# Layer seams worked one token block after the other, and a last quartet of expert pieces split by block

## The reference, cut to what matters

```
for i in range(4):                       # kinds: mla, swa, fox, mla
    y = branch_i(x) @ w_out_i
    x = layernorm(ALPHA * x + y, ln_g[i], ln_b[i])
# second family, one layer
h = rmsnorm(x, g_mix) * (1 + scale1) + shift1      # modulate
x = x + gate1 * (mix(h) @ w_out)                   # pooling and block attention, gated
h = rmsnorm(x, g_ffn) * (1 + scale2) + shift2
x = x + gate2 * peer(h)       # q = h @ w_q, top 16 of 128*128 experts per head,
                              # sum over experts of g * gelu(h . u[e]) * v[e]
out = rmsnorm(x, g_final)
```

## Time and profile before

| what | before |
|---|---|
| median of three runs | 1722.59 us |
| profiled execution | 1724.05 us, its span 1722.3 |
| TensorE busy | 1597.2 us, 93% |
| VectorE, ScalarE, GpSimd busy | 69%, 50%, 5% |
| DMA | 284.83 MB, mean 165 GB/s |

### The profile page before, as it was taken

How to read it: one execution, slowest core, us unless ns; L and a number is a source line. 1 busy time by engine, 2 the same in 40 slices (tenths; PEclk the granted TensorE clock), 3 DMA queues, 4 the chain that set the end, 5 groups by cost and what they waited for, 6 DMA issues and landing times.

```text
span 1722.3 us, 31048 instructions
## 1 busy us (share of the span) xinstructions
PE 1597.2 (93%) x10670; PEld 1376.5 (80%) x10670; DVE 1183.9 (69%) x2498; ACT 863.3 (50%) x1380; POOL 81.2 (5%) x110
## 2 busy tenths in 40 slices
PE   7888999899988887998799999899999999999996
PEld 6667967797767675876699999899999777778885
DVE  4665556556566656546547999787887999975554
ACT  4654354445446543444346666655655444444553
POOL 1120100100011210000000000000000000000000
PEclk9999999999999988988799999999999999999998
DMA  7544453455455454533354555544444444465552
GB/s 260 184 145 135 162 175 132 167 196 201 145 170 190 160 180 172 195 111 114 131 171 135 168 185 171 171 158 158 149 163 142 167 161 165 164 206 194 191 193 80
DMA packets 77172, 284.83 MB, mean 165 GB/s; under 512 B 9360, under 2 KB 9392, under 8 KB 75824
## 3 DMA queue, kind: packets, MB, share of 16 engines
q1 hardware_dynamic: 73280, 266.95, 46.2%
q0 software_dynamic: 3824, 16.99, 2.8%
HBM read 281.77 MB, written 2.14 MB: 165 GB/s over the span
## 4 chain that ended last, share of the span: by engine, by line
PE 77%; DVE 15%; ACT 4%; issue 3%; DMA 1%; DVEq 0%; ACTq 0%; POOLq 0%
PE banks L610 22%; PE banks L611 21%; PE banks L612 21%; DVE w_lo L1249 4%; PE banks L938 3%; PE banks L652 2%; PE banks L697 2%; PE banks L734 2%; PE banks L674 1%; DMA raw<-stream 1%; PE banks L746 1%; PE banks L745 1%; ACT scratch L1062 1%; DVE arena L1660 1%; ACT w_hi L996 1%
## 5 line engine op out<-in xcount | busy, mean ns | idle before, releaser
L1249 DVE TENSOR_TENSOR w_lo<-raw,w_hi 128x1024 fp32r<-128x1024 f32 x456 | 559.4, 1230 | 348.6 <-ACT w_hi L996 345.7
L996 ACT ACTIVATE w_hi<-raw 128x1024 fp32r<-128x1024 f32 x456 | 482.6, 1059 | 545.6 <-PE banks L612 521.5
L610 PE MATMUL banks<-w_hi,xT_hi 128*128 128x512 f32 (+2 forms) x1140 | 454.0, 398 | 12.7 <-DVE xT_lo L1281 6.6
L611 PE MATMUL banks<-w_lo,xT_hi 128*128 128x512 f32 (+2 forms) x1140 | 444.3, 390 | 0.0
L612 PE MATMUL banks<-w_hi,xT_lo 128*128 128x512 f32 (+2 forms) x1140 | 443.9, 389 | 0.0
L610 PE MATMUL banks<-xT_hi,w_hi 128*128 128x256 f32 x1360 | 392.8, 289 | 2.1 <-DVE arena L1301 1.2
L611 PE MATMUL banks<-xT_lo,w_hi 128*128 128x256 f32 x1360 | 386.8, 284 | 0.0
L612 PE MATMUL banks<-xT_hi,w_lo 128*128 128x256 f32 x1360 | 386.7, 284 | 0.0
L610 PEld LDWEIGHTS banks<-xT_hi,w_hi 128*128 128x128 f32 x1360 | 263.2, 194 | 3.6 <-issue 3.6
L610 PEld LDWEIGHTS banks<-w_hi,xT_hi 128*128 128x128 f32 x1140 | 218.0, 191 | 57.3 <-issue 10.5
L611 PEld LDWEIGHTS banks<-xT_lo,w_hi 128*128 128x128 f32 x1360 | 263.0, 193 | 0.0
(11 more groups left out here) (186 smaller groups left out, 1424.3 us busy)
## 6 DMA issues: line engine op xcount, KB each, us to landing
raw<-stream SPq DMA_DIRECT2D x504, 512.0 KB, 3.6
arena<-ln_in POOLq DMA_DIRECT2D x4, 1024.0 KB, 5.1
arena<-x_spill POOLq DMA_DIRECT2D x3, 1024.0 KB, 10.3
arena<-mod_rows POOLq DMA_DIRECT2D x2, 1536.0 KB, 8.3
arena<-g_in POOLq DMA_DIRECT2D x3, 512.0 KB, 8.6
arena<-x_in SPq DMA_DIRECT2D x1, 1024.0 KB, 5.0
arena<-bands_in POOLq DMA_DIRECT2D x1, 1024.0 KB, 5.4
arena<-keys_in POOLq DMA_DIRECT2D x1, 1024.0 KB, 5.3
```

Of the source, the lines that this page charges most:

```text
L610: pe.matmul(out, stationary[0], moving[0], start=first, stop=False, **k)
L611: pe.matmul(out, stationary[0], moving[1], start=False, stop=False, **k)
L996: act.activation(w_hi[:, s], half_raw(s), ACT.Copy).then_inc(piece_hi, 1)
L1249: dve.tensor_tensor(w_lo[:, s], half_raw(s), w_hi[:, s].bitcast(F32), ALU.subtract).then_inc(piece_lo, 1)
```

## The change

**Blocks instead of halves at the seams.** The second `out` unit becomes two: `project_closing` multiplies its four pieces for block 0 while all four stay in the ring, then for block 1, dropping each. VectorE closes block 0 by itself (`close_layer`: `take_block`, `norm_block`), between splits of pieces that stand at fixed places in its order, and then block 1. The next layer's first unit is opened in the same way: turn block 0, the row sums (`ada_rows`), three pieces for block 0, turn block 1, the fourth piece, then all four for block 1 (`open_layer`, `project_opening`). At the expert layer this first unit is a feature unit, whose matmuls then move 128 tokens each.

**Order of units.** Layer 1 starts with its first gate unit instead of the queries, layer 2 with its first value unit. The stream's order follows.

**The start.** The input comes as two loads; both engines split four pieces before they take the turned input.

**Roots.** ScalarE loads its table for the root ahead (`root_table`).

**The end.** The last four pieces are multiplied for block 0, then for block 1, each block closed by itself.

```
@@ plan @@
+        def closing_units(how):
+            first = Unit(plan, "token", [x_tok[:, b, 0:COLS] for b in range(B)], [("dve", how)] * B, pieces=4)
+            last = Unit(plan, "token", [x_tok[:, 0, COLS:D]], [("dve", how)], col0=COLS)
+            other = Unit(plan, "token", [x_tok[:, 1, COLS:D]], [("dve", how)], col0=COLS, pieces=4, pair=last.pair, at=1,
+                         after=(last.before,))
...
             elif kind == "swa":
+                L["gate"] = token_units(attn["gate"], D, SILU2, at=(0,))
                 L["q"] = feature_units(attn["qT"], KD, [("act", "scaled"), ("dve", "scaled")])
...
+                L["v"] = token_units(attn["v"], D, at=(0,))
+                L["q"] = feature_units(attn["qT"], KD)
...
@@ tensor @@
+            def project_closing(units):
+                for b, unit in enumerate(units):
+                    bank_free(unit)
+                    for n in range(RING):
+                        w = take_piece(n if b == 0 else 0)
+                        for kt in range(PK):
+                            mm = block_products(unit, b, [bank_of(unit, 0)], w, PK * n + kt, kt)
+                        if b:
+                            drop_piece(mm)
+                    if b == 0:
+                        mm.then_inc(unit_full, 1)
+
+            def project_opening(unit, turned, turn_other):
+                bank_free(unit)
+                for b in range(B):
+                    for n in range(RING):
+                        if n % 2 == 0:
+                            wait_put(pe, [turned[2 * b + n // 2]])
+                        if b == 0 and n == RING - 1:
+                            turn_other()
+                        w = take_piece(n if b == 0 else 0)
+                        bank = [bank_of(unit, b)] if unit.kind == "token" else [bank_of(unit, 0), bank_of(unit, 1)]
+                        for kt in range(PK):
+                            mm = block_products(unit, b, bank, w, PK * n + kt, kt)
+                        if b:
+                            drop_piece(mm)
...
+                turn_block(0)
+                if between is not None:
+                    between()
+                project_opening(unit, turned, lambda: turn_block(1))
...
-            with pe.Fori(0, HALF // RING) as i:
+            with pe.Fori(0, HALF // RING - 1) as i:
                 for s in range(RING):
                     second_table(RING * i + HALF, s)
+            for b in range(B):
+                for s in range(RING):
...
+                if b == 0:
+                    mm.then_inc(first_block, 1)
@@ scalar @@
+                if l == 0:
+                    split_ahead(0)
+                    for u in L["xT"]:
+                        evacuate_only(u)
...
+                pieces_behind(L["out"], 0)
+                root_table()
+                deviation(l, 0)
+                for n in range(1, RING):
+                    pieces_behind(L["out"], n)
...
@@ vector @@
+            def close_layer(l):
+                out, turned = layers[l]["out"], layers[l]["next"]
...
+                take_block(l, 0)
+                norm_block(l, 0)
+                pieces_behind(out, 1)
+                take_block(l, 1)
+                if l == DEPTH - 1:
+                    dve.wait_ge(x_half, 4 * l + 2)
+                    modulate_block(moba["h"], moba["mod"][:, 1], moba["mod"][:, 0], 0)
+                    norm_block(l, 1)
+                for u in turned[0:2]:
+                    evacuate_only(u)
+                pieces_behind(out, 3)
+                if l == DEPTH - 1:
+                    dve.wait_ge(x_half, 4 * l + 4)
+                    modulate_block(moba["h"], moba["mod"][:, 1], moba["mod"][:, 0], 1)
+                    dve.wait_ge(h_half, 4)
+                    dve.sem_inc(h_ready, 1)
+                else:
+                    norm_block(l, 1)
+                    dve.wait_ge(x_half, 4 * l + 4)
+                dve.sem_inc(ln_used, 1)
+                pieces_behind(out, RING)
+                for u in turned[2:4]:
+                    evacuate_only(u)
...
+            dve.wait_ge(first_block, 1)
+            close_end(0)
+            norm_end(0)
+            dve.wait_ge(piece_used, n_pieces)
+            close_end(1)
+            norm_end(1)
```

403 lines of the change are left out of this document (247 added, 156 removed).

## The result

The kernel after takes 1736.8 us in the median of 4 executions (1735.9 to 1738.2), the kernel before 1723.0: a ratio of 1.0074, with a 95% interval of 1.0044 to 1.0103. The record said 1708, between 1697 and 1717. So the change costs 14 us where 15 were forecast as a gain.

What follows compares the result with a forecast made beforehand. TensorE, busy 93% of the span, was taken as the bound, with time to regain only in holes, slow stretches and ends. Terms +5.8 -4.6 +0.9 -4.6 +6 -5.3 -8.6 +1.8 -6.1 gave -14.7 us: 1708, range 1697 to 1717.

Steps and rivals of the forecast that it cites:

- Staggered seams, layers 0 to 2: Handovers after layers 0 to 2: block-by-block work fills TensorE's idling; -4.6, -4.6, -5.3 us, each with 1 us charged for the clock.
- Layer 3's seam: Handover after layer 3, norm then modulation: block 0's modulation waits for block 1's statistics; gain 8.6 us, bounds 7 and 10.
- The expert seam: Handover to the expert layer: opening becomes 192 matmuls of 128 columns at 0.115 us, 22 us at full clock; loss 1.8 us.
- rival E: Four token openings: scattered waits keep the clock low, 192 matmuls at 0.43 in place of 0.23; 1742 us; chance 0.05.
- The start: Kernel start: four piece splits precede the turned inputs, first subtraction at 19.2, unit ends at 34.0; loss 5.8 us.
- Layer 2: Value unit moved ahead: VectorE waits about 7 us for the spread forget sums, TensorE idles 5, clock 2; loss 6 us.
- Layer 1's attention: Gate unit moved ahead in layer 1: scores wait for the keys' and values' evacuation, 0.2 + 0.69; loss 0.9 us.
- The end: Tail after the last matmul: block 0 closes under block 1's matmuls, 15.1 us becomes 9.0; gain 6.1 us.

Runs made afterwards that it cites:

- the second trace of the kernel after: The kernel after itself, run again unchanged for a second trace and more times: 1735.0 us, ratio 1.0104 to the kernel before.
- the filled wait: The kernel after with 12 extra 512-column matmuls, read by nobody, in the 2.91 us wait ahead of the expert block's narrow unit: 1718.5 us, ratio 0.9952.
- 384 in layer 2: The kernel before with layer 2's two key units made of 384 matmuls of 128 columns in place of 192 of 256: 1737.2 us, ratio 1.0085.
- staggered seam of layer 1: The kernel after with layer 1's old order of units, so that its opening is a query unit of 192 narrow matmuls: 1735.5 us, ratio 1.0089.
- the wide opening: The kernel after with both blocks turned first and the expert block's opening unit as 96 matmuls of 256 columns: 1714.6 us, ratio 0.9964.

## Why the prediction was wrong

**Staggered seams, layers 0 to 2: right.** Forecast -4.6 and +0.9 together, -4.6, -5.3; measured -5.2, -4.8, -5.6. At the first seam it was 28.2 us from the output unit's start to the end of the opening, not 28.45, and the waits were fewer (1 us, not 2). The charge of 1 us for each seam against the clock was not needed.

**Layer 3's seam: right in mechanism, 1.6 us short.** From the output unit's start to the next layer's second unit: 33.6 us, forecast 34.9; before 43.8, forecast 43.5. That makes 10.2 us for the seam; the other 3.5 of the table's 13.7 lie outside it, and come from the clock's falls in the trace of before: luck, since the second trace of the kernel after doesn't gain them. At the seam the clock came back during the row sums already and not in the opening unit.

**The expert seam: the step that decided.** Two steps of it held: the first wait (2.91, forecast 2.75) and the narrow matmul's price at full clock (0.115; measured 0.11). What failed is the step that gives half clock to the first of the eight quarter units ("some 5.1 (half clock), 3.1, 2.7") and full clock to the rest. All 192 ran at 1.2 GHz, 57.8 us from the output unit's start in place of 40.7, and 24 matmuls of the next unit too. The working had the clock rise after "about seven" matmuls at the seams of before, whose units move 256 or 512 columns, and carried it over to a form of which that trace had none. A clock that stays low through an opening unit was even on the list, as rival E at 0.05, but E put it into the four openings with 512 columns and left out the one seam where it came about.

For the price of a narrow matmul the Trainium skill, "TensorE: Matmul & The Clock Gate", section on the back-to-back issue gap, gives about 81 ns for a sustained pair with 128 columns. The rows here, fp32r parts at full clock, show 110 to 114 ns, and the measurement decides: the prediction was right to trust its own rows more than the page.

**The start: mis-sized.** +5.8 forecast, +10.9 measured. The first subtraction was to be done at 19.2 and was done at 21.2, since the splits of the last two pieces could begin at 17.1 only, and the fourth's not at 16.3 as before. Then the sum let TensorE multiply, and missed that the second half's turns wait for the first half's evacuation (one pair of banks), and that the first matmul comes behind them, at 23.96: 2.8 us more.

**Layer 2: right in each wait, short in the clock.** VectorE's wait was forecast as 7 us and was 6.58, TensorE's as 5 and was 4.28 (against 1.01 before). Charged for the clock were 2 us; at 0.50 for some 20 us it cost more: 9.7 in all against 6, and 18 in the kernel that changed the order alone. The bound of 8 was too low for the same reason: the return of the clock was priced as short.

**Layer 1's attention: left out.** The order was charged with its wait of 0.9 us (measured 0.83), and nothing for a clock that falls behind it: 7.9 us in this trace, and 47 to 59 us in place of 47 over all traces. Against rival E the prediction held that waits up to 1.1 us had left the clock at 0.98 in an attention stage; here waits of no more than that stood ahead of 20 us at 0.50. That the waits are the cause isn't shown.

**The end: right.** -6.1, measured -6.3 in the trace and -7.7 (interval 3.3 to 12) by itself.

Put together: the steps for queues, waits and durations came out within 2 us each, the start aside. What made a gain of 15 into a loss of 14 were 19 us at the expert seam and 8 and 4 in the two attention stages, nearly all of it time that TensorE spent at 1.2 GHz, and 5 at the start. Together these are some 35 us. On balance 8 us more than forecast were gained elsewhere, 6 of them by luck with the clock, so that the two traces differ by 12.3.

## What to carry to other kernels

After a change of a kernel that TensorE bounds, look at the granted clock of each stretch before its waits: here the time lost behind a wait of 1 to 4 us was 8 to 20 us. Don't let a unit of narrow matmuls follow a wait that brings the clock down: put wide ones first, or fill the wait with matmuls that nobody reads. And when work is moved nearer to its use, follow its result through every queue, for here a sum that left 11 us later against its use took the slack of 3.7 us with it.

## What the runs showed of the hardware

- A stream of 128x128 weights with 128 moving columns (fp32r, new weights for each) keeps the engine busy without a gap and yet did not bring the clock from 1.2 to 2.4 GHz: 192 of them, 41 us, in seven traces of the kernel after and its variants. The same stream kept 2.4 GHz where it began at 2.4 (192 behind the filled wait, 384 in layer 2, 192 behind the staggered seam of layer 1).
- Units of 256 columns came up about 5 us after their first matmul (852.36 to 857.3 in the wide opening, and 886.5 to 891.5 behind the narrow unit of the kernel after).
- Such a narrow matmul costs 0.11 us at 2.4 GHz and 0.213 at 1.2.
- Behind nine waits of 3.9 to 4.8 us at one point of layer 2, the clock stayed at 1.2 GHz for 3 to 34 us.
- The time of one and the same kernel, the one before, went from 1715.03 to 1736.81 us in 19 executions, with the mean clock between 0.963 and 0.949.
